# One-hot gather and scatter products of the expert layers as two fp32r passes each

## The reference, cut to what matters

```
def grouped_moe(h, router_w, router_b, w_gate, w_up, w_down):
    t = h.reshape(B * S, Dm)                       # 256 x 1024
    logits = t @ router_w + router_b               # 16 experts in 4 groups of 4
    ...                                            # best group by its two best probabilities,
    combine = jnp.sum(one_hot(top_idx, N_EXPERTS) * top_w[..., None], axis=1)
    for e in range(N_EXPERTS):
        hidden = silu(t @ w_gate[e]) * (t @ w_up[e])
        out = out + combine[:, e:e + 1] * (hidden @ w_down[e])
```

## Time and profile before

| | |
|---|---|
| median of 3 runs | 2644.69 us (2642.95 to 2645.48) |
| span of the profiled execution, first to last instruction | 2642.8 us |
| mean granted clock of PE over the span | 0.943 |
| PE / DVE / ACT / POOL busy, share of the span | 87% / 54% / 45% / 27% |
| first expert layer, from the table load to the end of the scatter | 276.22 to 624.61 us |
| second expert layer's scatter begins | 1313.8 us |

### The profile page before, as it was taken

How to read it: one execution, slowest core, us unless ns; L and a number is a source line. 1 busy time by engine, 2 the same in 40 slices (tenths; PEclk the granted TensorE clock), 3 DMA queues, 4 the chain that set the end, 5 groups by cost and what they waited for, 6 DMA issues and landing times. The chain is left out here.

```text
span 2642.8 us, 35172 instructions
## 1 busy us (share of the span) xinstructions
PE 2307.0 (87%) x11692; PEld 1834.7 (69%) x11692; DVE 1426.1 (54%) x2340; ACT 1200.1 (45%) x1832; POOL 702.3 (27%) x515
## 2 busy tenths in 40 slices
PE   7899699999798788999967757689999975799998
PEld 3884577774676647777654434389999975688886
DVE  1222588884423137888746872129990048655555
ACT  0450367771333306677511221235555569654554
POOL 0820000000574500000023710159999830000000
PEclk9999799999899888999988978799999999999999
DMA  8316388897443365888822101225555520255554
GB/s 333 128 65 251 138 327 331 330 347 268 174 175 128 128 231 218 329 320 335 324 100 105 48 32 64 103 82 181 184 182 187 185 87 0 96 191 193 195 191 151
DMA packets 66157, 491.25 MB, mean 186 GB/s; under 512 B 8353, under 2 KB 8993, under 8 KB 44321
## 3 DMA queue, kind: packets, MB, share of 16 engines
q1 hardware_dynamic: 64784, 482.45, 50.7%
q10 hardware_dynamic: 1296, 7.80, 0.8%
HBM read 489.18 MB, written 1.05 MB: 185 GB/s over the span
## 5 line engine op out<-in xcount | busy, mean ns | idle before, releaser
L981 DVE TENSOR_TENSOR moe_w_lo<-ring,moe_w_hi 128x1024 fp32r<-128x1024 f32 x384 | 454.2, 1221 | 53.5 <-ACT moe_w_hi L914 39.3
L914 ACT ACTIVATE moe_w_hi<-ring 128x1024 fp32r<-128x1024 f32 x384 | 390.9, 1057 | 64.2 <-PE bank L866 33.8
L2288 POOL TENSOR_TENSOR peer_u_lo<-peer_u,peer_u_hi 128x512 fp32r<-128x512 f32 x256 | 336.7, 1339 | 50.3 <-ACT peer_u_hi L2307 45.8
L2274 PE MATMUL bank<-peer_hn_hi,peer_u_hi 128*128 128x256 f32 x1024 | 292.1, 285 | 6.3 <-POOL peer_u_lo L2288 6.3
L2275 PE MATMUL bank<-peer_hn_lo,peer_u_hi 128*128 128x256 f32 x1024 | 287.1, 280 | 0.0
L2276 PE MATMUL bank<-peer_hn_hi,peer_u_lo 128*128 128x256 f32 x1024 | 286.8, 280 | 0.0
L221 POOL TENSOR_TENSOR ret_in_w_lo<-ring,ret_in_w_hi 128x1024 fp32r<-128x1024 f32 x48 | 117.3, 2457 | 510.8 <-ACT ret_in_w_hi L215 510.6
L847 PE MATMUL bank<-moe_w_hi,moe_slots_hi 128*128 128x512 f32 x512 | 209.5, 409 | 11.8 <-DVE moe_w_lo L981 7.9
L849 PE MATMUL bank<-moe_w_hi,moe_slots_lo 128*128 128x512 f32 x512 | 202.3, 395 | 0.0
L848 PE MATMUL bank<-moe_w_lo,moe_slots_hi 128*128 128x512 f32 x512 | 201.8, 394 | 0.0
L2274 PEld LDWEIGHTS bank<-peer_hn_hi,peer_u_hi 128*128 128x128 f32 x1024 | 193.5, 189 | 6.8 <-POOL peer_u_lo L2288 6.5
(11 more groups left out here) (460 smaller groups left out, 4565.3 us busy)
## 6 DMA issues: line engine op xcount, KB each, us to landing
ring<-in_stream SPq DMA_DIRECT2D x159, 2048.0 KB, 8.3
peer_u<-in_peer_u SPq DMA_DIRECT2D x128, 512.0 KB, 3.3
peer_v<-in_peer_v SPq DMA_DIRECT2D x128, 512.0 KB, 3.3
mod<-in_ada_b ACTq DMA_DIRECT2D x3, 1024.0 KB, 6.6
ring<-in_stream SPq DMA_DIRECT2D x2, 1024.0 KB, 5.1
mod<-in_ada_b ACTq DMA_DIRECT2D x1, 1536.0 KB, 15.4
mod<-in_ada_b ACTq DMA_DIRECT2D x3, 512.0 KB, 8.3
x<-in_x_tokens ACTq DMA_DIRECT2D x1, 1024.0 KB, 11.0
```

What stands on the lines that cost most here:

```text
L914: act.activation(w_hi[:, q, :], K.ring[:, at % RING, q * CHUNK // Q:(q + 1) * CHUNK // Q], ACT.Copy).then_inc(hi_done, 1)
L981: dve.tensor_tensor(w_lo[:, q, :], K.ring[:, at % RING, q * CHUNK // Q:(q + 1) * CHUNK // Q], w_hi[:, q, :].bitcast(F32), ALU.subtract).th ...
L2274: pe.matmul(out, u_hi[:, b, k2, :], h_hi[:, k, :], start=(k == 0), stop=False)
L2288: pool.tensor_tensor(u_lo[:, b, :, :], u[:, i, KD // 2 * half:KD // 2 * (half + 1), :], u_hi[:, b, :, :].bitcast(F32), ALU.subtract).then_ ...
```

## The change

`h` is split once per layer into `h_hi` (ACT) and `h_lo` (POOL), both fp32r; `hot` and `hotT` are written as fp32r. A gather product becomes two fp32r products, with the high and the low part of `h`. `y_all` becomes `y_hi` (ACT, the same copy in fp32r) and `y_lo` (a new subtraction on DVE, `take_low`), and a scatter product becomes two fp32r products. PE waits for `h_low` ahead of the first gather, and for `y_low` where it waited for `taken`. Transposes and the spreading of the weights keep reading `hot` as fp32. `take_low` stands behind the third quarter of `chunk(i, 1, 0)` on DVE, and behind the last chunk.

```diff
--- before.py
+++ after.py
@@ -679,10 +679,13 @@
         sb = lambda n, s, dt=F32: stage.enter_context(nc.sbuf_tensor(f"{name}_{n}", s, dt))
 
 
-        w_room = sb("w_room", [P, EXPERTS * T])
-        room = sb("room", [P, EXPERTS * T])
-        hot = sb("hot", [P, TT, GROUPS, P])
-        hotT = sb("hotT", [P, GROUPS, T])
+        with ExitStack() as dense:
+            w_room, room = (dense.enter_context(nc.sbuf_tensor(f"{name}_{n}", [P, EXPERTS * T], F32)) for n in ("w_room", "room"))
+        y_high_room, y_low_room = (sb(n, [P, EXPERTS * T], F32R) for n in ("y_high", "y_low"))
+        hot = sb("hot", [P, TT, GROUPS, P], F32R)
+        hotT = sb("hotT", [P, GROUPS, T], F32R)
+        h_hi, h_lo = (sb(n, [P, TT, D], F32R) for n in ("h_hi", "h_lo"))
+        h_high, h_low, y_low = (s_(s) for s in ("h_high", "h_low", "y_low"))
         eq = sb("eq", [P, TT, P])
         gated_s, hidden_s = sb("gated_s", [P, COLS]), sb("hidden_s", [P, COLS])
         slot_w = sb("slot_w", [P, EXPERTS])
@@ -789,7 +792,7 @@
             s_(s) for s in ("made", "spread_w", "hot_ready", "wide", "gathered", "slots_h", "slots_l"))
         hi_done, lo_done, q_used, turned, hid_h, hid_l, taken = (
             s_(s) for s in ("hi", "lo", "q_used", "turned", "hid_h", "hid_l", "taken"))
-        y_all = w_room[:].rearrange("p (g d) -> p g d", g=GROUPS)
+        y_hi, y_lo = y_high_room[:].rearrange("p (g d) -> p g d", g=GROUPS), y_low_room[:].rearrange("p (g d) -> p g d", g=GROUPS)
         LAST_DOWN = n_end - 1 - n0
 
 
@@ -806,6 +809,7 @@
         def tensor_gathered(pe):
             pe.sem_inc(q_used, Q)
             pe.wait_ge(hot_ready, TT)
+            pe.wait_ge(h_low, 1)
 
             def gather(i):
 
@@ -815,21 +819,22 @@
                             one = hot[:, tt, 0, :]
                         else:
                             one = hot[:, tt, bass.ds(i + 1, 1), :].rearrange("p o s -> p (o s)")
-                        last = pe.matmul(K.bank[:, 2 + k // 4, k % 4 * P:(k % 4 + 1) * P], h[:, tt, k * P:(k + 1) * P],
-                                         one, start=(tt == 0), stop=(tt == 1))
+                        for part in (h_hi, h_lo):
+                            last = pe.matmul(K.bank[:, 2 + k // 4, k % 4 * P:(k % 4 + 1) * P], part[:, tt, k * P:(k + 1) * P],
+                                             one, start=(tt == 0 and part is h_hi), stop=(tt == 1 and part is h_lo))
                 last.then_inc(gathered, 1)
 
             gather(None)
             for g in range(GROUPS):
                 for tt in range(TT):
                     last = pe.transpose(K.bank[:, 4 + g // 2, (g % 2) * T + tt * P:(g % 2) * T + (tt + 1) * P],
-                                        hot[:, tt, g, :], K.ident)
+                                        hot[:, tt, g, :].bitcast(F32), K.ident)
             last.then_inc(made, 1)
             pe.wait_ge(weights_ready, 1)
             for g in range(GROUPS):
                 mine = slice(g * PER_GROUP, (g + 1) * PER_GROUP)
                 for tt in range(TT):
-                    last = pe.matmul(K.bank[:, 6, mine], hot[:, tt, g, :], comb[:, tt, mine], start=(tt == 0), stop=(tt == 1))
+                    last = pe.matmul(K.bank[:, 6, mine], hot[:, tt, g, :].bitcast(F32), comb[:, tt, mine], start=(tt == 0), stop=(tt == 1))
             last.then_inc(spread_w, 1)
 
             def quarters(c, product):
@@ -886,7 +891,7 @@
                     up_product(i, r, 1)
                     if r < PER_GROUP - 1 and (i is not None or r):
                         if r == 1 and i is not None:
-                            pe.wait_ge(taken, i + 1)
+                            pe.wait_ge(y_low, i + 1)
                         down_product(chunk(i, r, 2), e, (r - 1) % PER_GROUP)
 
             experts(None)
@@ -895,12 +900,14 @@
             down_product((LAST_DOWN - 1, 0), EXPERTS - 1, PER_GROUP - 2)
             turn_hidden(EXPERTS)
             down_product((LAST_DOWN, 0), EXPERTS, PER_GROUP - 1)
-            pe.wait_ge(taken, GROUPS)
+            pe.wait_ge(y_low, GROUPS)
             for tt in range(TT):
                 for dh in range(2):
                     for g in range(GROUPS):
-                        pe.matmul(K.bank[:, 2 * tt + dh, :], hotT[:, g, tt * P:(tt + 1) * P],
-                                  y_all[:, g, dh * 512:(dh + 1) * 512], start=(g == 0), stop=(g == GROUPS - 1))
+                        for part in (y_hi, y_lo):
+                            last = pe.matmul(K.bank[:, 2 * tt + dh, :], hotT[:, g, tt * P:(tt + 1) * P],
+                                             part[:, g, dh * 512:(dh + 1) * 512], start=(g == 0 and part is y_hi),
+                                             stop=(g == GROUPS - 1 and part is y_lo))
 
         def scalar_gathered(act):
             def high(c, after=None):
@@ -937,7 +944,7 @@
             def take(g, done):
 
                 act.wait_ge(q_used, done)
-                out = y_all[:, g, :] if isinstance(g, int) else y_all[:, bass.ds(g, 1), :].rearrange("p o d -> p (o d)")
+                out = y_hi[:, g, :] if isinstance(g, int) else y_hi[:, bass.ds(g, 1), :].rearrange("p o d -> p (o d)")
                 act.activation(out, K.bank[:, 6:8, :].rearrange("p b c -> p (b c)"), ACT.Copy).then_inc(taken, 1)
 
             slots_high(None)
@@ -1004,6 +1011,14 @@
                 w = slot_w[:, e:e + 1] if isinstance(e, int) else slot_w[:, bass.ds(e, 1)]
                 dve.scalar_tensor_tensor(hidden_s[:], K.bank[:, 1, :], w, gated_s[:], ALU.mult, ALU.mult).then_inc(hidden_done, 1)
 
+            def take_low(g, count):
+
+                dve.wait_ge(taken, count)
+                high, out = (a[:, g, :] if isinstance(g, int) else a[:, bass.ds(g, 1), :].rearrange("p o d -> p (o d)")
+                             for a in (y_hi, y_lo))
+                dve.tensor_tensor(out, K.bank[:, 6:8, :].rearrange("p b c -> p (b c)"), high.bitcast(F32),
+                                  ALU.subtract).then_inc(y_low, 1)
+
             slots_low(None)
             dve.wait_ge(spread_w, 1)
             c_.do(dve.tensor_copy(slot_w[:], K.bank[:, 6, 0:EXPERTS]))
@@ -1015,6 +1030,8 @@
                         low(chunk(i, -1, 2), {1: lambda: slots_low(i), 2: lambda: make_hidden(i, -1, PER_GROUP * i + (PER_GROUP - 1))})
                     if r == 1 and i is None:
                         low(chunk(i, r, 0), {1: lambda: make_hidden(None, 0, 0)})
+                    elif r == 1:
+                        low(chunk(i, r, 0), {2: lambda: take_low(i, i + 1)})
                     else:
                         low(chunk(i, r, 0))
                     low(chunk(i, r, 1), {1: lambda: hidden_low(e)} if i is not None or r else None)
@@ -1026,6 +1043,7 @@
                 experts(i)
             low((LAST_DOWN - 1, 0), {1: lambda: make_hidden(None, PER_GROUP - 1, EXPERTS - 1, (LAST_DOWN - 2, 0))})
             low((LAST_DOWN, 0), {1: lambda: hidden_low(EXPERTS)})
+            take_low(GROUPS - 1, GROUPS)
 
 
         w_all = w_room[:].rearrange("p (e t) -> p e t", e=EXPERTS)
@@ -1162,8 +1180,14 @@
                 with pe.Else():
                     tensor_gathered(pe)
 
+            @block.gpsimd
+            def _(pool):
+                pool.wait_ge(h_high, 1)
+                pool.tensor_tensor(h_lo[:], h[:], h_hi[:].bitcast(F32), ALU.subtract).then_inc(h_low, 1)
+
             @block.scalar
             def _(act):
+                act.activation(h_hi[:], h[:], ACT.Copy).then_inc(h_high, 1)
                 act.wait_ge(exp_ready, 1)
                 act.activation(ex[:], pr[:], ACT.Exp).then_inc(exp_made, 1)
                 act.wait_ge(exp_ready, 2)
```

## The result

The changed kernel takes 2646.69 us (median of 19 runs, 2643.94 to 2652.55), the kernel before 2642.95 us in the same sessions (19 runs, 2638.14 to 2645.48). The ratio is 1.0016, 95% interval 1.001 to 1.0023. By the 0.2% line of the prediction that is "within"; the forecast was 2638.8, 0.22% faster. The sign was wrong: not -5.9 us but some +4. The time lies inside the stated range of 2630 to 2675, but only in the room made for the rivals A and D, whose mechanisms did not occur.

What follows compares the result with a forecast made beforehand. The prediction took the expert layers as bound by PE, with DMA close behind. Tails -10.4, take_low in the loop +4.9 and gathers -0.4 gave -5.9 us, so 2638.8 us was forecast, range 2630 to 2675.

Steps and rivals of the forecast that it cites:

- 0.2% line: Whole kernel: a measurement can tell about 0.2%, 5.3 us, from no change; a result within it had chance 0.28.
- A: Rival for the gathers, chance 0.22: an fp32r product with few moving columns is slow, +31 us, together 2670.
- D: Rival, chance 0.08: loop take_low costs 1.3 us and upsets hid_lo, or tail handovers are slower; 2642 to 2648.
- Scatter: Tail of each layer: 32 records 0.2265 us apart instead of 0.429, a gain of 6.5 us a layer.
- The second copy in the tail: Tail: PE waits for the new take_low subtraction on DVE behind ACT's copy, a cost of 1.26 us a layer.
- take_low in the loop: Three a layer: DVE's new subtraction makes the fourth w_lo quarter start 0.8 us late for PE, +4.9 in all.
- Gather: Eight gathers: the record count stays and each costs 0.11 to 0.115 us, so -0.05 us each, -0.4 in all.
- C: Rival for the gathers, chance 0.12: column count rules and they get cheaper, -14.4 us, together 2624.
- The work under cover: Block's start: splitting h on ACT and POOL has twelve microseconds of slack and costs 0.
- The sum: Whole kernel: -10.4 + 4.9 - 0.4 = -5.9 us, a forecast of 2638.8 us, 0.22% less.

Runs made afterwards that it cites:

- E2: Changed kernel with h, hot and the gather back in fp32, only the scatter in two fp32r passes: 2637.45 us, ratio to before 0.9985.
- E3: Changed kernel with the first gather of each layer back in fp32, the three in the loop in fp32r: 2637.58 us, ratio to before 0.9983.
- E4: Changed kernel with take_low in the loop behind the second quarter of w_lo instead of the third: 2642.38 us, ratio to before 1.0.
- E7: Changed kernel with five spare fp32 products of 256 columns behind the branch, ahead of the first gather: 2643.46 us, ratio to before 1.001.
- E9: Changed kernel with five spare fp32 products of 256 columns ahead of the branch before the first gather: 2641.67 us, ratio to before 0.9995.
- E1: Kernel before with only h, hot and the gather changed; scatter, y_all and take stay fp32: 2647.13 us, ratio to before 1.0018.
- E5: Changed kernel with ten spare fp32r products of 512 columns ahead of PE's last wait for y_low: 2643.75 us, ratio to before 1.001.
- E6: Changed kernel with the scatter's groups 0 to 2 ahead of the last wait for y_low: 2637.24 us, ratio to before 0.9987.
- E8: E2 with the edits of E4 and E6: 2630.17 us, ratio to before 0.9957.
- E10: E8 with the five spare products of E9 ahead of the branch: 2628.3 us, ratio to before 0.9943.

## Why the prediction was wrong

- **Scatter, priced at -6.5 a layer by its spacing.** The spacing was right (0.2265 us, the same 32 records). What went missing was the clock: 9.1 and 9.2 us instead of 7.4, behind a wait of 2.4 us instead of 1.1. In 11 of the 12 tails of the six changed variants that leave this wait in place (the changed kernel, E2, E3, E4, E7, E9) the scatter takes 9.0 to 9.2 us, in one 7.6, and with the wait filled 7.6 in both. Net of the handover a tail gave 3.6 us and not 5.2.
- **The second copy in the tail, +1.26.** Right: idle 2.37 against 1.11.
- **take_low in the loop, +0.8 each.** Right, 0.9: +5.4 for +4.9. Place and mechanism hold, by the trace and by E4.
- **Gather, "-0.05 us each", eight of them.** Right for the six in the loop, where nothing moved (3.52 against 3.49): rivals A and C, a short fp32r record that is slow or cheap, are both out. Wrong for the first of each layer, and this is the step that turned the sign. I took "the first gather of a layer starts at half clock and takes 5.97" as a property of the place, and let it and everything behind it keep their times. The row is an average over half clock and full (0.62): the fp32 gather was raised while it ran, the fp32r one was not. The term was as good as 0 (-0.1 for two layers) and measured +7.9. E1 shows that the gather alone brings it, E2 and E3 that two fp32 gathers take it away, and the second layer of E9 that the clock and not the passes makes it. In all ten expert layers of the runs whose first gather is fp32r with nothing spare ahead (the changed kernel, E1, E4, E5, E6) R to G1 is 90.5 to 92.2, and in the eight with an fp32 gather and nothing spare (before, E2, E3, E8) 86.6 to 87.8. The granted clock over that gather and the small products behind it is 0.50 throughout in all the ten; in all the eight it rises during the gather and is full behind it.
- **The work under cover** cost nothing, as said.
- **The sum.** Expected -10.4 + 4.9 - 0.4 = -5.9; by the trace -7.2 + 5.4 + 7.9 = +6.1, by the ratio about +4.2. By the marks the span should have grown by 6.1 and grew by 2.1; the rest lies in stretches that the change doesn't touch, and no run settles it further. No rival had the clock; A forecast the right sign for a reason that didn't occur. D's 2642 to 2648 holds the measured time, but by luck: its terms, take_low at 1.3 us and a slower handover in the tail, came out at 0.9 and as priced. One sum of the prediction is off without weight: C's -14.4 gives 2625 and not 2624.

Why the fp32r gather leaves the clock low with the same number of records stays open. The two differ in what a record costs at 512 columns (0.429 us in fp32, 0.2265 in fp32r), not at 128 (0.11 in both), and no run varies this by itself. The Trainium skill, "TensorE: Matmul & The Clock Gate", section "What's actually happening", says that the gate follows how busy PE has recently been. The traces agree in part: the spare work of E7 and of E9's second layer raised the clock. But the profile lists PE as busy throughout both gathers (5.96 of 6.00 us and 7.08 of 7.10), so its busy time doesn't tell them apart, and the same spare work failed in E9's first layer.

## What to carry to other kernels

Here cheaper matmuls paid where they have many columns and a full clock (the scatter, from 14.0 us to 7.4 where its wait was filled). Where a record costs the same in either type (128 columns, 0.11 us) two passes brought nothing, and right behind an idle stretch they left PE at half clock, which cost 7.9 us, most of it in the unchanged work behind them. When a row mixes two clocks, ask what raised it. Look for the neighbour's hole before placing a new instruction, and move finished parts of a sum into the last wait.

## What the runs showed of the hardware

- A product of 128x128 weights and 128 columns costs the same in fp32 per record and in fp32r per pass: 32 take 3.8 us at full clock in fp32r (E9's second layer) and 3.81 (E10) or 3.73 in fp32.
- PE stood idle for 2.37 us at the tail, behind dense work, and the granted clock fell to half (1.2 GHz) as the scatter began and stayed there for its first 3.3 us or so (0.53 in that window); behind 1.11 us of idling it stayed at 2.4 GHz in both layers of before. With the long wait this was so in 11 of 12 tails, not in all, and by the spacing of the records and the granted clock the fall came between 0.3 us ahead of the scatter's start (E2, second layer) and 1.3 us behind it (E4, first layer).
- Two gathers of 32 records, with the same cost per record at full clock, don't do the same to the clock: the fp32 one was raised while it ran in all eight heads of that kind with nothing spare ahead, the fp32r one in none of ten. Of 3.3 us lost in the first head of the changed kernel 1.1 lie in the gather, the rest in the work behind it.
- Five spare products, 4.6 us of PE's time ahead of the branch, raised the clock in one layer of E9 and both of E10, and not in the other layer of E9: such a cure is not certain.
